# A mixture of 32 experts on one core: a new layout of the experts' weights and columns, and the last chunk loaded in two parts

## The reference

```python
logits = xt @ w_router + b_router                 # 256 tokens, 32 experts
top_val, top_idx = lax.top_k(logits, TOP_K)       # TOP_K = 4
gates = softmax(top_val)
# for each expert e and each token routed to it:
hdn = xb @ w_up[e] + b_up[e]                      # 1024 -> 2048
gate_h = minimum(hdn[:, :1024], 7.0)
up_h = clip(hdn[:, 1024:], -7.0, 7.0)
act = (up_h + 1.0) * gate_h * sigmoid(1.702 * gate_h)
y = (act @ w_down[e] + b_down[e]) * gate          # 1024 -> 1024
# y is added to its token's row; then a layer norm and a gated projection
```

## Time and profile before

| | us |
|---|---|
| median of 3 runs | 2349.51 (2348.63 to 2351.63) |
| profiled execution, span from first to last instruction | 2345.1 |
| PE busy | 2265.2 (97%) |
| DVE, ACT, POOL busy | 815.0, 499.8, 154.2 |
| DMA, mean over the span | 257 GB/s |

### The profile page before, as it was taken

How to read it: one execution, slowest core, us unless ns; L and a number is a source line. 1 busy time by engine, 2 the same in 40 slices (tenths; PEclk the granted TensorE clock), 3 DMA queues, 4 the chain that set the end, 5 groups by cost and what they waited for, 6 DMA issues and landing times.

```text
span 2345.1 us, 34269 instructions
## 1 busy us (share of the span) xinstructions
PE 2265.2 (97%) x14376; PEld 1662.3 (71%) x14376; DVE 815.0 (35%) x2072; ACT 499.8 (21%) x1180; POOL 154.2 (7%) x162
## 2 busy tenths in 40 slices
PE   7999999999999999999999999999999999999998
PEld 4777888888887788887688845666665555565556
DVE  2245554578425420005664321222222222222224
ACT  3255411100024432002443211111111111111113
POOL 1000111144301000000000000000000000000000
PEclk9999999999999999999999999999999999999999
DMA  9733223234325444344332777999999999999993
GB/s 376 276 108 108 108 72 108 72 126 162 108 84 200 182 177 148 144 150 180 131 143 109 295 288 310 426 427 425 427 427 426 427 427 426 427 426 426 427 426 124
DMA packets 44196, 601.60 MB, mean 257 GB/s; under 512 B 4704, under 2 KB 7392, under 8 KB 7808
## 3 DMA queue, kind: packets, MB, share of 16 engines
q1 hardware_dynamic: 43696, 595.40, 62.8%
q10 hardware_dynamic: 336, 3.87, 0.4%
HBM read 598.20 MB, written 1.05 MB: 256 GB/s over the span
## 4 chain that ended last, share of the span: by engine, by line
PE 82%; DMA 13%; DVE 2%; ACT 2%; issue 1%; POOL 0%; SPq 0%; POOLq 0%; PEldq 0%; DVEq 0%; ACTq 0%
PE PS L1203 14%; PE PS L957 8%; PE PS L1227 8%; DMA RG<-in_w_up 7%; PE PS L702 7%; PE PS L737 6%; PE PS L686 5%; PE PS L789 5%; DMA BIG<-in_w_up 4%; PE PS L650 3%; PE PS L535 3%; PE PS L775 2%; PE PS L1239 2%; PE PS L1132 2%; PE PS L474 2%; PE PS L1331 1%
## 5 line engine op out<-in xcount | busy, mean ns | idle before, releaser
L2560 DVE TENSOR_SCALAR STAT<-PS 128x128 f32<-128x128 f32 (+1 forms) x128 | 37.9, 296 | 668.4 <-PE PS L1203 668.4
L1203 PE MATMUL PS<-BIG,XS 128*64 128x256 f32 (+1 forms) x2016 | 236.3, 384 | 6.1 <-DMA BIG<-in_w_up 6.1
L1203 PEld LDWEIGHTS PS<-BIG,XS 128*64 128x64 f32 (+1 forms) x2016 | 145.2, 138 | 95.1 <-issue 17.9
L1203 PE MATMUL PS<-RG,XS 128*64 128x256 f32 (+1 forms) x1520 | 178.0, 384 | 12.2 <-DMA RG<-in_w_up 10.2
L957 PE MATMUL PS<-XS,RG 128*128 128x256 f32 x768 | 172.1, 382 | 5.0 <-DVE XS L1997 4.1
L1382 ACT ACTIVATE BIG<-PS 128x256 f32<-128x256 f32 (+2 forms) x197 | 82.2, 432 | 441.9 <-PE PS L702 138.9
L1203 PEld LDWEIGHTS PS<-RG,XS 128*64 128x64 f32 (+1 forms) x1520 | 107.9, 137 | 80.4 <-DMA RG<-in_w_up 15.8
L957 PEld LDWEIGHTS PS<-XS,RG 128*128 128x128 f32 x768 | 145.5, 191 | 26.9 <-issue 6.9
L1846 ACT ACTIVATE STAT<-STAT 128x128 f32<-128x128 f32 (+1 forms) x128 | 40.1, 313 | 570.2 <-DVE STAT L2560 570.2
L1963 DVE TENSOR_SCALAR HOLD<-PS 128x256 f32<-128x256 f32 x27 | 11.4, 423 | 382.0 <-PE PS L510 277.9
L686 PE MATMUL PS<-HN,RG 128*128 128x256 f32 x576 | 125.1, 379 | 1.0 <-ACT HN L1431 1.0
(11 more groups left out here) (374 smaller groups left out, 3427.9 us busy)
## 6 DMA issues: line engine op xcount, KB each, us to landing
BIG<-in_w_up SPq DMA_DIRECT2D x64, 2048.0 KB, 30.5
RG<-in_w_up SPq DMA_DIRECT2D x48, 2048.0 KB, 31.3
BIG<-in_w_down SPq DMA_DIRECT2D x32, 2048.0 KB, 32.0
RG<-in_w_ff SPq DMA_DIRECT2D x31, 2048.0 KB, 8.1
RG<-in_w_ada SPq DMA_DIRECT2D x24, 2048.0 KB, 8.3
RG<-in_w_down SPq DMA_DIRECT2D x24, 2048.0 KB, 34.5
RG<-in_w_in SPq DMA_DIRECT2D x23, 2048.0 KB, 8.2
SM<-in_w_up SPq DMA_DIRECT2D x16, 2048.0 KB, 31.3
```

What stands on the lines that cost most here:

```text
L1203: i = pe.matmul(half_of(b, h, sides), Xg[:, k, 0:cap], w[:, k, h * wd:h * wd + wd], start=False, stop=k == 7)
```

## The change

**Chunks.** An up chunk now holds half of the rows of k (4 tiles of 128) and half of the output columns, as 2 x 512; two chunks make one bank. A down chunk holds half of the rows and all 1024 output columns. Every matmul of up and down in a narrow expert is 512 columns wide. The bytes of a chunk are the same.

**Gather.** SEL holds four experts at once (4 x 64 columns). The product is made the other way around (line 1141: HTM's columns are the weights, SEL moves, 256 wide) and comes out upright, so the four `upright` transposes and one copy are gone. Each expert gathers one quarter of the width (j = ex % 4) for the next four; ahead of expert 0 three quarters are gathered at once, and the fourth between its first two chunks. DVE's SEL compares with POS + 1, which is 0 where the token isn't routed.

**Broad.** The capacity is 96: all 64 places as in the narrow body, and 32 more in matmuls of 32 columns (`more_up`, `more_down`, 16 per chunk), four beside each other, with a gather, biases, activation, transposes and a scatter of their own. The dense path is taken above 96 tokens in place of 128.

**Order.** An expert's scatter and the wait for its copy move behind the next expert's biases. The two copies to YV become one of 512 columns. The lower biases are 8 matmuls on four groups of 32 rows, ahead of the first expert; the transposed gates are made in four groups of rows for them.

**Last chunk.** Chunk 191 is issued as two transfers of 1 MB. PE waits for the first at the chunk's beginning, and for the second ahead of its third tile of k.

```diff
+            def gather(key, j):
+                b = take(("xg",) + key)
+                for i in range(2):
+                    for tt in range(2):
+                        m = pe.matmul(banks[b][:, 256 * i:256 * i + 256], HTM[:, tt, 256 * j + 128 * i:256 * j + 128 * i + 128],
+                                      SEL[:, tt, :], start=tt == 0, stop=tt == 1)
+                m.then_inc(s_full[b], 1)
+            def upper_biases(ex):
+                for s in range(2):
+                    b = take(("up", ex, s), quiet=True)
+                    for h in range(2):
+                        q = 2 * s + h
+                        rows = slice(32 * q, 32 * q + 32)
+                        pe.matmul(banks[b][64 * h:64 * h + 64, :], ID2[rows, 32 * q + ex:32 * q + ex + 1].broadcast_to([32, 64]),
+                                  BUPR[rows, :], start=True, stop=False)
+            def more_up(b, c, w):
+                xg = XG2.rearrange("p (k s) -> p k s", k=8)
+                for kk in range(4):
+                    for q in range(4):
+                        part = w[:, kk, 512 * (q // 2):512 * (q // 2) + 512].rearrange("p (g n) -> p g n", g=2)
+                        m = pe.matmul(banks[b][32 * q:32 * q + 32, 256 * (c // 2):256 * (c // 2) + 256], xg[:, 4 * (c % 2) + kk, :],
+                                      part[:, :, 128 * (q % 2):128 * (q % 2) + 128], start=False, stop=c == 3 and kk == 3,
+                                      skip_group_check=True)
+                return m
...
+                upper_biases(ex)
...
+                if broad:
+                    more_picked(ex, b2)
+                if ex:
+                    scatter(ex - 1)
+                    read_out(("xg", ex - 1))
...
+                    for kk in range(4):
...
+                        for h in range(2):
+                            i = pe.matmul(banks[b][64 * h:64 * h + 64, :], XG[:, 4 * (c % 2) + kk, 64 * r:64 * r + 64],
+                                          w[:, kk, 512 * h:512 * h + 512], start=False, stop=c % 2 == 1 and kk == 3)
...
+                    if broad:
+                        if c == 0:
+                            pe.wait_ge(s_mcopy, 7 * ex + 2)
+                        i = more_up(b3, c, w)
                     i.then_inc(s_used, 1)
...
+                if broad:
+                    pe.wait_ge(s_mcopy, 7 * ex + 3)
                 if ex + 1 < NEXP:
+                    pe.wait_ge(s_sel, 2 + min(ex, NEXP - 5))
+                    gather((ex,), ex % 4)
...
+                        if ex == NEXP - 1 and c == 1 and kk == 2:
+                            pe.wait_ge(s_landed[R.slot["expert", ex, 5]], 16 * R.nth["expert", ex, 5])
```

```diff
             def select(ex):
-                if ex:
-                    full(("xt", ex - 1))
-                for tt in range(2):
-                    i = dve.tensor_scalar(SEL[:, tt, 0:64], IOTA[:, 0:64], POS[:, tt, ex:ex + 1], MSK[:, tt, ex:ex + 1],
-                                          ALU.is_equal, ALU.mult)
-                i.then_inc(s_sel, 1)
+                dve.tensor_tensor(SEL[:, :, 64 * (ex % 4):64 * (ex % 4) + 64], IOTA[:, 0:64].rearrange("p (o s) -> p o s", o=1).broadcast_to([128, 2, 64]),
+                                  POS[:, :, ex:ex + 1].broadcast_to([128, 2, 64]), ALU.is_equal).then_inc(s_sel, 1)
...
-            dve.tensor_scalar(FLAG[0:1, 32:33], SV[0:1, 410:411], 128.0, None, ALU.is_gt).then_inc(s_flag, 1)
+            dve.tensor_scalar(FLAG[0:1, 32:33], SV[0:1, 410:411], 96.0, None, ALU.is_gt).then_inc(s_flag, 1)
...
                 if i >= 8:
                     sp.wait_ge(s_used, i - 7)
-                landing(key, source(key))
+                if i == 6 * NEXP - 1:
+                    sp.dma_start(ring(R.slot[key])[:, 0:2048], source(key)[:, 0:2048]).then_inc(s_first, 16)
+                    sp.dma_start(ring(R.slot[key])[:, 2048:4096], source(key)[:, 2048:4096]).then_inc(s_landed[R.slot[key]], 16)
+                else:
+                    landing(key, source(key))
```

More of the change, by code:

```diff
@@ new lines, in activated, with scatter @@
+            def activated(b, s):
+                for i in range(2):
+                    m = pe.transpose(banks[b][:, 128 * i:128 * i + 128], AV[:, 256 * s + 128 * i:256 * s + 128 * i + 128], ID2)
+                m.then_inc(s_full[b], 1)
+            def scatter(ex):
+                read_out(("sc", ex))
+                read_out(("dn", ex))
+                for j in range(4):
+                    for h in range(2):
+                        rows = slice(64 * h, 64 * h + 64)
+                        m = pe.matmul(accap(4 * h + j), YV[rows, 128 * j:128 * j + 128], SCT[rows, :], start=False,
+                                      stop=ex == NEXP - 1, skip_group_check=True)
+                m.then_inc(s_scat, 1)
@@ new lines, in more_biases @@
+            def more_biases(ex, b):
+                pe.wait_ge(s_free[b], F.n[b])
+                for s in range(2):
+                    for q in range(4):
+                        g = 2 * s + q // 2
+                        bias = BUPR.rearrange("p (g n) -> p g n", g=2)[:, :, 128 * (q % 2):128 * (q % 2) + 128]
+                        pe.matmul(banks[b][32 * q:32 * q + 32, 256 * s:256 * s + 256],
+                                  ID2[:, 32 * g + ex:32 * g + ex + 1].broadcast_to([128, 32]), bias, start=s == 0, stop=False,
+                                  skip_group_check=True)
@@ L1169, in expert, with more_scatter @@
+            def more_scatter(ex):
+                pe.wait_ge(s_mcopy, 7 * ex + 7)
+                for j in range(2):
+                    for q in range(4):
+                        rows = slice(32 * q, 32 * q + 32)
+                        pe.matmul(accap(2 * q + j), YV2[rows, 128 * j:128 * j + 128], TS2[rows, 256:512], start=False, stop=False,
+                                  skip_group_check=True)
             def expert(ex, broad):
-                Xg = XG[ex % 2]
-                cap = 128 if broad else 64
@@ L1172, in expert @@
[L1172 to L1173 removed]
+                r = ex % 4
                 if ex + 1 < NEXP:
@@ L1279, in _ @@
                     read_out(("ht", tt, half))
-            gather(0)
+            pe.wait_ge(s_sel, 1)
+            for j in range(3):
+                gather(("first", j), j)
             pe.wait_ge(s_flag, 1)
@@ L1352, in _ @@
                     pe.wait_ge(s_free[b], taken[b])
-                for d in range(8):
-                    pe.matmul(accap(d), BD[0:32, d * 128:d * 128 + 128], GTT, start=d % 2 == 0, stop=False, skip_group_check=True)
                 for ex in range(NEXP):
@@ L1863, in dense @@
                     act.activation(SG[:, f % 2, :], GH[:, f % 2, :], ACT.Sigmoid, scale=1.702).then_inc(s_dsg, 1)
-            gathered(0)
+            for j in range(3):
+                gathered(("first", j), j)
             act.wait_ge(s_flag, 1)
```

337 lines of the change are left out of this document (176 added, 161 removed).

## The result

The changed kernel took 2333.49 us (2330.68 to 2334.39, 4 runs); the kernel before, beside it, 2349.07 us (2346.01 to 2351.63, 4 runs). Ratio 0.9933, interval 0.9919 to 0.9948: **15.6 us faster**, where 8.1 against the runs beside it were forecast. 2341.0 us was too slow by 7.5 us, and the result lies 1.0 us under the range. The span of the profiled execution went from 2345.1 to 2332.6 us, -12.5.

The account below looks back on a forecast made before the run. PE was taken to bound the head up to chunk 20, weight transfers the stream after it. Head -4.6, stream -4.8, tail +0.95 gave -8.45: span 2336.65, plus 4.4 to the median, 2341.0 us; range 2334.5 to 2349.

Parts of the forecast that it names:

- odd steps: In the weight stream, extra delays of 1.36 us, one with every eighth instruction packet; four or five expected in place of eight.
- The head's steps: PE's work from the first gather to expert 2's first weights, priced piece by piece; sum -4.6 us for chunk 20.
- transition: PE's passage from an expert's up to its down in the head: -0.75 us in expert 0, +2.95 in expert 1.
- Of the chunk behind it I keep everything, a PE stall of 2.03 us without a releaser too: Expert 2's first weights chunk, at the head's end: its time, with a 2.03 us PE stall, was taken as unchanged.
- The stream: The 171 weight chunks behind chunk 20: 33 instruction packets in place of 57, -4.8 us, between 0 and -6.8.
- The tail: The end of expert 31, with one later copy to YV and a longer DVE chain: +0.95 us (0.5 to 1.5).
- the split saves nothing: Last chunk in two transfers: no gain, as PE reaches it when landed; otherwise half a chunk, 1.72 us.
- From span to median I carried 4.4 us: The kernel before's median of 2349.5 us lies 4.4 above its profiled span; the same was added to the forecast span.
- more than I forecast: Rival: the broad expert's 32-column pieces at 1.7 us and seven stream delays gone, 2337 us; chance 0.12.
- x: Price per up chunk of the broad expert's other 32 places, 16 matmuls of 32 columns; taken as 2.0 us.
- Serial biases: Rival: upper-bias matmuls paired to one bank run one after the other, +2.35 us three times in the head, 2348.1; chance 0.08.
- The slower rival: Rival: expert 1's 32-column pieces do not run beside each other, 6.9 us each, +21 us, 2370.5; chance 0.04.

Follow-up runs that it names:

- a_halves: The changed kernel with every 512-wide matmul of up, down and the upper biases as two of 256: 2345.3 us, ratio 0.9997 to the kernel before.
- a_down_halves: The changed kernel with only the matmuls of down as two of 256 columns: 2342.32 us, ratio 0.9984 to the kernel before.
- a_one_piece: The changed kernel with the last chunk as one transfer of 2 MB with one wait: 2330.94 us, ratio 0.994 to the kernel before.
- a_same: The changed kernel run again without any edit: 2333.5 us, ratio 0.9943 to the kernel before.
- a_moved: The changed kernel with experts 1 (the broad one) and 24 renamed into each other: 2317.58 us, ratio 0.9865 to the kernel before.
- a_pool48: The changed kernel with 12240 semaphore increments more on idle POOL, 72 per chunk: 2422.97 us, ratio 1.033 to the kernel before.
- b_moved12: The kernel before with the broad expert's number exchanged with number 12: 2322.23 us, ratio 0.99 to the kernel before.
- b_moved: The kernel before with experts 1 (the broad one) and 24 renamed into each other: 2350.12 us, ratio 1.0012 to the kernel before.
- a_late_moved: The changed kernel with experts 1 and 24 exchanged and the lower biases between experts 11 and 12: 2320.76 us, ratio 0.9876 to the kernel before.

## Why the prediction was wrong

Its mechanisms held, and the rivals of another sign didn't come about. Three terms of the sum were mis-sized, all in one direction: a stall for code that was kept, the number of odd steps in the stream, and what was carried from the span to the median.

- **The head's steps** were right, to 0.5 us each and 0.9 in sum. Each as forecast, then measured, in us: ahead of expert 0 +2.9, +3.1 (its own start 0.22 later, apart from 1.0 by which the part ahead of the stage was later in this execution); expert 0's up +1.25, +1.25; transition -0.75, -0.95; ahead of expert 1 -1.75, -1.85; its up -7.05, -7.04; transition +2.95, +2.44; down -2.75, -2.84; behind +0.6, +0.44. With that 1.0 they give -4.5 for expert 2's start (1430.41), for which -4.6 stood. That these two agree so closely is luck: the steps were 0.9 better than forecast, and the part ahead of the stage 1.0 later.
- **"Of the chunk behind it I keep everything, a PE stall of 2.03 us without a releaser too"** failed. The chunk took 3.69 us (1430.41 to 1434.10) in place of 6.38: -2.7, of which the stall is 2.03 and the rest isn't traced. A stall for code is no property of the work, and a change that rewrites the code ahead of it should have had a range for it, from 0 to what one costs: a_halves shows 2.09 and 2.34 us in two places, a_down_halves 4.33 in one, the changed kernel none. Of the 7.2 us by which chunk 20 is issued earlier, 7.1 reach the fastest engine and 5.8 the landing, since the slowest engine is 2.24 us behind there in place of 0.96.
- **The stream** (-4.8, at most -6.8) is mis-sized: -7.3. The count of packets was nearly right (33 forecast, 31 measured), and so was the rule of an odd step at every eighth of them, as the steps of the gap show. The step that failed is "four or five odd steps of 1.36 us in place of eight": three came. 31 packets make 3.9 steps of eight, and which of them fall between chunk 20 and chunk 191 depends on the count at its start; a fourth was due eight packets behind the third, just as chunk 191 landed. Before, the first of the eight fell two chunks behind chunk 20; in the changed kernel the gap had grown to 2.24 us ahead of it, so that 1.3 of the 7.3 us are a matter of where the line between head and stream is drawn. On average 27 packets at 0.17 to 0.2 us are worth 4.6 to 5.4 us, near the forecast; the rest is how the steps happened to fall. So the 7.3 us are no price for 27 packets elsewhere.
- **The tail** (+0.95) measured +0.6, and the split saves nothing, as said: 0.2 us between a_one_piece and a_same. PE reaches the last chunk at 2284.85, when its first half has long landed (2282.49) and the second is 0.13 us away.
- **From span to median I carried 4.4 us**; 0.9 was right (2333.49 against 2332.6). The execution shown of before was a quick one, about 2.2 us under its median, and the change was then summed against it; that of the changed kernel came out 0.9 above its own. With the 1.8 us by which all later executions exceed their spans, the forecast would have been 2338.5. This is the largest item of the miss and no mechanism of the kernel: from execution to execution the times differ by more.
- In sum: head 1.2 more than forecast (landing of chunk 20), stream 2.5, tail 0.35, median 3.5: 7.5 us.
- **A sum of its own that doesn't agree.** The rival "more than I forecast" (x at 1.7, seven steps gone) was put at 2337. Its terms give 2334.5, as the range's lower end says: 1.8 us for x, and 4.7 for three and a half steps more.
- **Serial biases**, the rival that the Trainium skill stands behind (TensorEngine Tiling (Array Packing), Gotcha 1: PSUM Pressure), gave 2348.1. Eight records of 512 take 1.09 us where in a row they would take 3.45, so this trace does not agree with the rule where the partitions written differ (here 0 to 63 and 64 to 127).
- **The slower rival** priced the 32-column pieces at 6.9 us; 1.93 was measured, pitch 1.87, for which 2.0 stood. DVE's second chain let PE wait 2.28 and 0.79 us in expert 1, inside the forecast 6.9.

The undoing fits: a_halves gives back the 4.3 us of the stream and 6.0 in the head, 4.4 of these in stalls for code, and is level with the kernel before (0.9985 to 1.0008). So without the 512-wide matmuls the gather, the order and the 96 columns save no more, with these inputs, than the stalls for code take. The 512-wide matmuls gain by less code, not by faster work: the same up chunk takes 3.65 us with them and 3.67 without. Which layout of the code is free of stalls is luck as far as these runs tell.

The best version measured is a_moved, 2317.58 us, 16 us under the changed kernel, for inputs whose busy expert is known.

## What to carry to other kernels

When a stream of weights runs at the limit of the DMA engines, count the packets of code in the same stretch, and measure how far a transfer's first and last increment drift apart: that gap is what the stream loses, and fewer, wider instructions win it back (here 12.8 us at the end with 58 packets, 6.7 with 31). Price a stall without a releaser as something that the next change may remove or move, never as a constant, and give it a range. Put the one long piece of work where a full ring and enough slack behind it hide it, and not beside other extra work: in the kernel before the same expert cost some 24 us at the start and almost nothing in the middle, and all of it again at number 24, where it met the lower biases, a stall of 6.42 us and few experts behind it to catch up. And before a change is summed against one profiled execution, see where this one lies among the times of its kernel.

## What the runs showed of the hardware that was not expected

- Instructions that do nothing, on an engine without work, slowed the whole kernel: 6120 semaphore increments on POOL by 25 us, 12240 by 89, of which 58 in the stream. Their packets (8 KB, queue q14) all delay one of the 16 DMA engines, 0.57 us each in the first, though a packet's own time is 0.32 us. PE's packets (16 KB, queue q8, 1.07 us each) spread over eight or nine engines, as I read the increments.
- The delay of one engine builds up silently: in a_pool48 bandwidth stayed at 427 GB/s until the gap was about as long as six buffers, and only then fell to some 400. A ring that runs dry lets the slow engines catch up (5.01 to 2.11 us in b_moved12).
- Matmuls of 32 rows in different row groups, written in pairs to one bank on different partitions, overlap: 1.09 us for 8 records of 512, where the prediction worked out 3.45 for one after the other.
- PE stalls for code of 1.67 to 6.42 us stand in seven of the kernels, at places that change with the layout of the code. Behind the longest two, among others, the granted clock fell to its lower level, 1.2 GHz (0.50 between 2045 and 2055 us in b_moved; 0.78 on average between 2080 and 2090 us in a_late_moved), and where PE is then behind the stream, that delay stays to the end.
